# Scan stage: the three taps of each projection's shift placed apart, two R pieces behind a correction

## The chip, the cores and the metric

The kernel runs on one core of one Trainium2 chip. The metric is the device time of one execution in microseconds (us), and the median of the runs is compared. An execution of the kernel before takes about 3002 us; the profile is that of one further execution.

## What is computed

The kernel computes two transformer blocks on 512 tokens of 1024 channels. The change touches one stage of the first block only, the token mixer's recurrent scan. Cut to what matters:

```python
def centred_shift(z, w):                      # three taps along the tokens
    zp = jnp.pad(z, ((0, 0), (1, 1), (0, 0)))
    return zp[:, :-2] * w[0] + zp[:, 1:-1] * w[1] + zp[:, 2:] * w[2]

z = h @ p["w_in"]                             # r, k, v of every head, of 512 tokens and 256 context tokens
r, k, v, ... = split(centred_shift(z_rwkv, shift_conv))
def step(S, inp):                             # generalised delta rule, forward and reverse, per head
    s_kk = einsum('bhvk,bhk->bhv', S, kk_t)
    S_new = S * d_t - s_kk * (kk_t * a_t) + v_t * k_t
    y = einsum('bhvk,bhk->bhv', S if reverse else S_new, r_t)
```

After the scan come its readout, a gated merge, a mixture of experts, and the second block (two attention mixers). They are the same in both kernels.

## The kernel before

`stage_scan` treats the 1024 channels as 8 blocks of 128 (two heads each). The tokens are cut in 12 steps of 64 (4 of context, 8 of the sequence), in both directions. Inside a step the recurrence is turned into a triangular system; its inverse is built for groups of 4 steps by 5 levels of correction. Between steps a 64x64 state is carried.

**Turns and slots.** The loop runs over turns j = 0 to 8. A turn has three groups s of five levels l, so 15 corrections, each with two half slots; the text writes a half slot as (s, l, 0) or (s, l, 1), and a correction as (s, l). A turn takes about 100 us. In it three channel blocks are in work: j gets its inverses, the state steps go through the end of block j-1 (s = 0) and the beginning of j, and block b = j+1 is prepared: its projections, shifts, decays, rates and scores. For b to exist j is 0 to 6.

**One correction, on four engines.** All instruction streams are written out by hand and run in their written order; they meet at semaphores. PE: `product` (it waits for the inverse of the level before), the right side of a state step with the scores beside it, then what `beside(j, (s, l, 0))` gives, `solve` (waits for the negated right side), `correct` (waits for the mask), `read_out` (waits for the copied solution), then `beside(j, (s, l, 1))`. DVE: `mask` (L1548), `beside` 0, `update` (L1559 of X, L1561 of XT), `state` (L1574, and L1578 for the scaled ZG), `beside` 1. ACT: `negate` (L1218), `beside` 0, `solved` (L1223), `beside` 1. In a group's last level PE runs `correct_last` (L825, and L828, which turns the next group's start matrix XT); L828 waits for POOL's `xt0`, two instructions (L1476, L1478), and these wait for ACT's `part_moved` (L1276, two instructions), which waits until DVE's `parts` has masked all scores of that group's steps.

**Projections and shifts.** PE projects block b in pieces (L684; the context's K and V at L680) into one PSUM bank, in the order K_X, K_V, R_X, V_X; the next projection waits until the shift of the one before has read the bank. DVE's `shift(b, which)` reads the bank with three taps: a product (L400, for K_V L1604), and two multiply-adds (L403, L406; for K_V L1607, L1610). Each counts a semaphore, `shift`. K_V is two parts of 256 tokens, so its taps are six instructions; the others have three on 512 tokens. Behind the last tap of K_V wait ACT's `square(b)` (L1287, 128x768, in half slot (1, 2, 1)), POOL's reversal of v and PE's R_X projection.

**Where things stand before.** On DVE: `parts(j, 4..11)` one each in (s, 0..3, 0) for s = 0, 1; `shift(b, K_X)` in (0, 3, 0); `shift(b, K_V)` in (1, 2, 1); `gated(a)` (L1725) in (1, 3, 0); `parts(b, 0)`, `parts(b, 2)` (L1638) and `shift(b, R_X)` in (2, 2, 1); `scaled_r(b)` in (2, 3, 1). On PE: pieces 0 and 1 of R_X in (1, 3, 0), `squares(b)` (L695) in (1, 3, 1), piece 2 in (1, 4, 0). On ACT: `square(b)` in (1, 2, 1), `part_moved(j, 2)` in (1, 3, 1), `part_moved(b, 0)` in (2, 3, 0), ahead of `solved` of that slot, `part_moved(j, 1)` in (0, 3, 1).

Of the kernel before, what the change touches and what calls it, by code (L numbers as in the profile page):

```python
# [7 lines left out]
ALU = mybir.AluOpType  # L8
# [4 lines left out]
T, TC, D = 512, 256, 1024  # L13
# [383 lines left out]
def shifted(own, dve, parts, w):  # L397

    for dst, z, n in parts:
        own.then(dve.tensor_scalar(dst, z, w[1], None, ALU.mult))  # L400
    own.settle()
    for dst, z, n in parts:
        own.then(dve.scalar_tensor_tensor(dst[:, 1:n], z[:, 0:n - 1], w[0], dst[:, 1:n], ALU.mult, ALU.add))  # L403
    own.settle()
    for dst, z, n in parts:
        own.then(dve.scalar_tensor_tensor(dst[:, 0:n - 1], z[:, 1:n], w[2], dst[:, 0:n - 1], ALU.mult, ALU.add))  # L406
    own.settle()
# [106 lines left out]
def stage_scan(k, hT, w_low, low_loaded, th, da, sg, ya, spare, m, first_chunk, first_loaded, loose):  # L514
# [20 lines left out]
    with ExitStack() as s:  # L535
# [70 lines left out]
        SHIFTED = 15  # L606
# [20 lines left out]
        def _(pe):  # L627
# [363 lines left out]
            def beside(j, at):  # L991

                a, b = j - 1, j + 1
                if at == (0, 0, 0):
                    turn_params(b)
                if at == (0, 0, 1):
                    project(b, K_X, 0)
                if at == (0, 1, 0):
                    project(b, K_X, 1)
                    bonus(j)  # L1000
                if at == (0, 1, 1):
                    project(b, K_X, 2)
                if at == (0, 2, 1):
                    project(b, K_X, 3)
                if at == (0, 2, 0):
                    both_directions(b, "rate")
                if at == (0, 3, 0):
                    both_directions(b, "decay")
                if at == (0, 3, 1):
                    to_tokens(j, "B", 0)  # L1010
                if at == (0, 4, 0):
                    context_of(b, 0)
                    to_tokens(j, "K", 0)
                if at == (0, 4, 1):
                    context_of(b, 1)
                    center(a)
                    project(b, K_V, 0)
                if at == (1, 0, 0):
                    variance(a)
                if at == (1, 0, 1):  # L1020
                    project(b, K_V, 1)
                if at == (1, 1, 0):
                    project(b, K_V, 2)
                    spread_rstd(a)
                if at == (1, 1, 1):
                    project(b, K_V, 3)
                if at == (1, 2, 1):
                    gate(a)
                if at == (1, 3, 0):
                    project(b, R_X, 0, KT)  # L1030
                    project(b, R_X, 1, KT)
                if at == (1, 3, 1):
                    squares(b)
                if at == (1, 4, 0):
                    project(b, R_X, 2, KT)
                if at == (1, 4, 1):
                    project(b, R_X, 3, KT)
                if at == (2, 0, 0):
                    spread_inverse(b)
                if at == (2, 0, 1):  # L1040
                    project(b, R_X, 4, KT)
                if at == (2, 1, 0):
                    project(b, R_X, 5, KT)
                if at == (2, 1, 1):
                    project(b, R_X, 6, KT)
                if at == (2, 2, 0):
                    project(b, R_X, 7, KT)
                if at == (2, 2, 1):
                    scores(b, 0)
                    scores(b, 2)  # L1050
                if at == (2, 3, 1):
                    for i in range(3):
                        project(b, V_X, i, KT)
                if at == (2, 4, 0):
                    for i in range(3, 5):
                        project(b, V_X, i, KT)
                if at == (2, 4, 1):
                    for i in range(5, KT):
                        project(b, V_X, i, KT)
# [480 lines left out]
        def _(dve):  # L1540
# [43 lines left out]
                    sc.settled(dve, "par", j)  # L1584
                    ts(col(j, 18), col(j, 10), -1.0, 1.0, ALU.mult, ALU.add).then_inc(S["par_done"], 1)

            def shift(j, which):

                if not live(j):
                    return  # L1590
                dve.wait_ge(S["proj"], proj_no(j, which))
                mine = Steps(dve, S["shift"], shift_no(j, which - 1) if which else SHIFTED * j)
                taps_of = lambda i: [col(j, 3 * t + i) for t in range(3)]
                z_of = proj_bank(j, which)
                if which == K_X:
                    if j:
                        dve.wait_ge(S["ke_done"], 2 * j)
                    shifted(mine, dve, [(kj[:, XS], z_of[:], T)], taps_of(1))
                elif which == K_V:
                    if j:  # L1600
                        sc.settled(dve, "tokV", j - 1, 0)
                    parts_ = ((kj[:, CS], z_of[:, 0:TC], taps_of(1)), (vj[:, CS], z_of[:, TC:2 * TC], taps_of(2)))
                    for dst, z, w in parts_:
                        mine.then(ts(dst, z, w[1], None, ALU.mult))  # L1604
                    mine.settle()
                    for dst, z, w in parts_:
                        mine.then(stt(dst[:, 1:TC], z[:, 0:TC - 1], w[0], dst[:, 1:TC], ALU.mult, ALU.add))  # L1607
                    mine.settle()
                    for dst, z, w in parts_:
                        mine.then(stt(dst[:, 0:TC - 1], z[:, 1:TC], w[2], dst[:, 0:TC - 1], ALU.mult, ALU.add))  # L1610
                    mine.settle()
                elif which == R_X:
                    shifted(mine, dve, [(rj[:], z_of[:], T)], taps_of(0))
                else:
                    if j:
                        sc.settled(dve, "tokV", j - 1, 1)
                        sc.settled(dve, "tokV", j - 1, 2)
                    shifted(mine, dve, [(vj[:, XS], z_of[:], T)], taps_of(2))

            def bonus(j):  # L1620
                if live(j):
# [104 lines left out]

            def beside(j, at):
                a, b = j - 1, j + 1
                if at[0] < 2 and at[1] < 4 and at[2] == 0:
                    parts(j, 4 + 4 * at[0] + at[1])  # L1730
                if at == (0, 0, 0):
                    params(b)
                if at == (0, 1, 1):
                    bonus(j)
                if at == (0, 3, 0):
                    shift(b, K_X)
                if at == (1, 0, 0):
                    inverse_deviation(a)
                if at == (1, 0, 1):
                    running_sums(b, 0)  # L1740
                if at == (1, 1, 1):
                    normed(a)
                if at == (1, 2, 1):
                    shift(b, K_V)
                if at == (1, 3, 0):
                    gated(a)
                if at == (1, 3, 1):
                    clamp(b)
# [10 lines left out]
                    scaled_q(b, 0)  # L1759
                if at == (2, 2, 1):  # L1760
                    parts(b, 0)
                    parts(b, 2)
                    shift(b, R_X)
                if at == (2, 3, 1):
                    scaled_r(b)
                if at == (2, 4, 0):
# [1919 lines left out]
```

## Time and profile before

| | us |
|---|---|
| median of 3 runs | 3002.47 (3000.74 to 3004.83) |
| the profiled execution's own time | 3004.26 |
| its span, first to last instruction | 3002.5 |
| scan, turns 0 to 7 | about 125 to 908 on the span's clock |

The page of the profile gives busy shares over the span: PE 91%, DVE 39%, ACT 20%, POOL 8%. In the timeline a row has the start, the duration, the engine (PE matmul, PEld weight load, DVE, ACT, POOL), the line and operation, how many instructions are merged in the row, and in brackets the idle time ahead of it with what ended it ("<-DVE vj L1610": an instruction of DVE at line 1610 that wrote vj). "issue" is idle time for which the profile shows no wait. [...]

### The profile page before, as it was taken

What the parts mean: (1) busy time and instruction counts of PE and PEld (TensorE: products, weight loads), DVE (VectorE), ACT (ScalarE), POOL (GpSimd) and SP (SyncE); (2) the same over time, 40 slices, a digit from 0 to 9 for tenths busy, and PEclk for the clock granted to TensorE, in tenths of its full rate; (3) what the DMA queues carried; (4) which work ended last, traced back from release to release, by engine and by line L of the source; (5) the groups of instructions that cost most, each with busy time, mean ns of one, the idle gap of its engine ahead of it and who ended that gap; (6) DMA issues with size and microseconds to landing.
All of it is one profiled execution on the core that took longest, in us unless ns stands there. A gap on an engine that the chain in (4) does not pass through costs nothing. (4 is left out here: it accounts for less than half of the span.)

```text
span 3002.5 us, 69531 instructions
## 1 busy us (share of the span) xinstructions
PE 2732.5 (91%) x31106; PEld 1482.5 (49%) x31106; DVE 1182.1 (39%) x2613; ACT 608.2 (20%) x1255; POOL 250.1 (8%) x282
## 2 busy tenths in 40 slices
PE   6899999999999899988998989989887999899998
PEld 3566666776664445444433433433333455455553
DVE  3565566566643673163221211212013245423333
ACT  3233233333321100010000000000002344322222
POOL 1121122112200000001000000000000021110000
PEclk9999999999999999998999999999997999999999
DMA  5000000000005773167999999999995421042210
GB/s 204 24 26 14 19 26 20 21 19 26 12 26 196 279 282 113 56 273 297 430 431 431 430 431 430 431 431 430 431 431 196 134 71 37 0 123 63 63 42 29
DMA packets 191501, 557.42 MB, mean 186 GB/s; under 512 B 32140, under 2 KB 119714, under 8 KB 166646
## 3 DMA queue, kind: packets, MB, share of 16 engines
q1 hardware_dynamic: 191222, 553.19, 47.0%
q8 instruction: 237, 3.88, 0.5%
q14 instruction: 42, 0.34, 0.0%
HBM read 550.65 MB, written 2.24 MB: 184 GB/s over the span
## 5 line engine op out<-in xcount | busy, mean ns | idle before, releaser
L2327 PE MATMUL bank<-arena,xe 128*64 128x512 f32 x1024 | 345.2, 601 | 35.0 <-DMA gates<-in_exp_w_dram 24.0
L684 PE MATMUL bank<-arena 128*128 128x512 f32 x384 | 201.5, 647 | 6.7 <-DVE vj L1610 5.3
L2327 PEld LDWEIGHTS bank<-arena,xe 128*64 128x64 f32 x1024 | 107.9, 138 | 183.1 <-issue 170.4
L3354 PE MATMUL bank<-arena 128*128 128x512 f32 x384 | 176.2, 607 | 3.4 <-PEq L3232 3.4
L2327 PE MATMUL bank<-arena,hidT 128*64 128x512 f32 x512 | 171.7, 599 | 2.4 <-DMA gates<-in_exp_w_dram 1.9
L2780 PE MATMUL bank<-arena 128*128 128x512 f32 x320 | 143.3, 596 | 0.0
L2327 PE MATMUL bank<-mg_ring,xe 128*64 128x512 f32 x256 | 117.9, 615 | 20.9 <-DMA u<-in_exp_w_dram 20.9
L2552 DVE TENSOR_TENSOR x<-x,bank 128x512 f32<-128x512 f32 x64 | 43.7, 686 | 227.6 <-PE bank L2365 227.6
L2545 DVE TENSOR_TENSOR hid<-hid,bank 128x512 f32<-128x512 f32 x32 | 19.8, 682 | 285.4 <-PE bank L2327 285.4
L2327 PE MATMUL bank<-ys,xe 128*64 128x512 f32 x256 | 114.5, 600 | 19.1 <-DMA arena<-in_exp_w_dram 18.5
L1548 DVE TENSOR_TENSOR pm<-bank,m_level 128x512 f32<-128x512 f32 x120 | 82.7, 689 | 118.1 <-PE bank L763 117.1
L843 PE MATMUL bank<-pm,XT 64*64 64x32 f32 x3072 | 107.0, 219 | 12.6 <-DVE pm L1548 10.7
L2327 PE MATMUL bank<-u,xe 128*64 128x512 f32 x256 | 118.2, 616 | 0.0
L2327 PE MATMUL bank<-gates,xe 128*64 128x512 f32 x256 | 117.9, 615 | 0.0
L845 PE MATMUL bank<-XT,pm 64*64 64x32 f32 x3072 | 110.8, 221 | 1.7 <-issue 1.7
L3354 PEld LDWEIGHTS bank<-arena 128*128 128x128 f32 x384 | 70.9, 192 | 84.0 <-issue 84.0
L763 PEld LDWEIGHTS bank<-X,px 64*64 64x64 f32 x2560 | 84.9, 134 | 49.5 <-issue 22.5
L843 PEld LDWEIGHTS bank<-pm,XT 64*64 64x64 f32 x3072 | 99.7, 136 | 17.1 <-DVE pm L1548 12.9
L763 PE MATMUL bank<-X,px 64*64 64x64 f32 x2560 | 97.1, 223 | 7.5 <-issue 4.8
L845 PEld LDWEIGHTS bank<-XT,pm 64*64 64x64 f32 x3072 | 99.5, 135 | 0.6 <-issue 0.5
L684 PEld LDWEIGHTS bank<-arena 128*128 128x128 f32 x384 | 67.8, 197 | 63.7 <-issue 57.9
L183 DVE SCALAR_TENSOR_TENSOR arena<-ws_w,silu_c,arena 128x512 f32<-128x512 f32 x120 | 90.2, 752 | 12.5 <-DMA ws_w<-in_ada_w_dram 7.5
(530 smaller groups left out, 5471.7 us busy)
## 6 DMA issues: line engine op xcount, KB each, us to landing
arena<-in_exp_w_dram SPq DMA_DIRECT2D x96, 2048.0 KB, 26.8
gates<-in_exp_w_dram SPq DMA_DIRECT2D x24, 2048.0 KB, 29.6
ys<-in_exp_w_dram SPq DMA_DIRECT2D x24, 2048.0 KB, 26.7
mg_ring<-in_exp_w_dram SPq DMA_DIRECT2D x24, 2048.0 KB, 25.7
u<-in_exp_w_dram SPq DMA_DIRECT2D x24, 2048.0 KB, 30.2
ws_w<-in_ada_w_dram SPq DMA_DIRECT2D x40, 1024.0 KB, 5.2
arena<-in_odd_w_in_dram SPq DMA_DIRECT2D x32, 512.0 KB, 3.9
arena<-in_w_in_dram SPq DMA_DIRECT2D x24, 512.0 KB, 4.2
```

Of the source, the lines that this page charges most:

```text
L183: own.last(dve.scalar_tensor_tensor(acc, w, factor, acc, ALU.mult, ALU.add))
L684: last = mm(to[:], wj[:, c, i, :], hT[:, c, 0:T], start=(c == 0), stop=(c == KT - 1))
L763: last = mm(INV[c, cs(q)], part(4 * g + q // 2, q % 2, 0, 0)[h], X[h, (j * GROUPS + g) % 2, q, :], start=True, stop=True)
L843: mm(into(INV, h, q), XT[c, g, q, :], blocks(pm[c, q, :], b, 0), start=True, stop=True)
L845: last = mm(into(INVT, c, q), pm[c, q, :], blocks(XT[c, g, q, :], b, 1), start=True, stop=True)
L1548: tt(pm[:], INV[:].rearrange("p (q t) -> p q t", q=8), m["level"][:, l, :].unsqueeze(1).to_broadcast([P, 8, HEAD]), ALU.mult).then_inc(S[" ...
L2327: r[e] = mm(out[a, :], lhs[j][:, a], w[:, j, 512 * c:512 * c + 512], start=(first and j == 0), stop=(last and j == len(lhs) - 1), skip_gro ...
L2545: dve.tensor_tensor(hid[:, f, :], hid[:, f, :], bank[4 + f][:], ALU.mult).then_inc(S["hid_made"], 1)
L2552: dve.tensor_tensor(x1[:, n, c], x1[:, n, c], bank[scatter_bank(q, o)][:], ALU.add).then_inc(S["added"], 1)
L2780: last = mm(o[:], w[:, c, i, :], hT[:, i, :], start=(i == 0), stop=(i == KT - 1))
L3354: last = mm(o[:], w[:, i, t, :], hT[:, t, :], start=(t == 0), stop=(t == KT - 1))
```

## The change

Nothing is computed otherwise; instructions of DVE and PE stand in other places.

- DVE's `shift` takes the taps to be done. K_X: tap 0 in (0, 2, 1), tap 1 in (0, 3, 0), tap 2 in (0, 3, 1). K_V: tap 0 in (1, 2, 0), tap 1 in (1, 2, 1), tap 2 in (1, 3, 0), ahead of `gated(a)`. R_X: taps 0 and 1 in (2, 2, 1), tap 2 in (2, 3, 0). V_X and the prologue keep all three together.
- DVE's `parts(j, 11)` goes from (1, 3, 0) to (1, 3, 1), `parts(b, 2)` from (2, 2, 1) to (2, 3, 0), behind tap 2 of R_X.
- PE's pieces 0 and 1 of R_X go from (1, 3, 0), ahead of `solve` and `correct`, to (1, 3, 1), behind them and ahead of `squares(b)`.

```diff
@@ PE, beside
-                if at == (1, 3, 0):
+                if at == (1, 3, 1):
                     project(b, R_X, 0, KT)
                     project(b, R_X, 1, KT)
-                if at == (1, 3, 1):
                     squares(b)
@@ DVE, shift
-            def shift(j, which):
+            def shift(j, which, taps=range(3)):
...
+                mine = Steps(dve, S["shift"], (shift_no(j, which - 1) if which else SHIFTED * j) + taps[0] * len(parts_))
+                if taps[0] == 0:
+                    dve.wait_ge(S["proj"], proj_no(j, which))
...
+                for tap in taps:
+                    if tap:
+                        mine.settle()
+                    for dst, z, w, n in parts_:
+                        if tap == 0:
+                            mine.then(ts(dst, z, w[1], None, ALU.mult))
+                        elif tap == 1:
+                            mine.then(stt(dst[:, 1:n], z[:, 0:n - 1], w[0], dst[:, 1:n], ALU.mult, ALU.add))
+                        else:
+                            mine.then(stt(dst[:, 0:n - 1], z[:, 1:n], w[2], dst[:, 0:n - 1], ALU.mult, ALU.add))
+                mine.settle()
@@ DVE, beside
-                if at[0] < 2 and at[1] < 4 and at[2] == 0:
+                if at[0] < 2 and at[1] < 4 and at[2] == (1 if at[0:2] == (1, 3) else 0):
                     parts(j, 4 + 4 * at[0] + at[1])
...
+                if at == (0, 2, 1):
+                    shift(b, K_X, (0,))
                 if at == (0, 3, 0):
-                    shift(b, K_X)
+                    shift(b, K_X, (1,))
+                if at == (0, 3, 1):
+                    shift(b, K_X, (2,))
...
+                if at == (1, 2, 0):
+                    shift(b, K_V, (0,))
                 if at == (1, 2, 1):
-                    shift(b, K_V)
+                    shift(b, K_V, (1,))
                 if at == (1, 3, 0):
+                    shift(b, K_V, (2,))
                     gated(a)
...
                 if at == (2, 2, 1):
                     parts(b, 0)
+                    shift(b, R_X, (0, 1))
+                if at == (2, 3, 0):
+                    shift(b, R_X, (2,))
                     parts(b, 2)
-                    shift(b, R_X)
```

## Rows read from the trace of the kernel before

**Rows 1.** The page, part 1: engine, busy us (share), instructions.
```profile
PE 2732.5 (91%) x31106; PEld 1482.5 (49%) x31106; DVE 1182.1 (39%) x2613; ACT 608.2 (20%) x1255; POOL 250.1 (8%) x282
```

**Rows 2.** Busy time by stretch, turn 6: us, engines in order, granted clock.
```profile
727.00:825.00 98.00, 91.84 (x2781) 67.32 (x2777) 61.63 (x126) 34.01 (x70) 18.77 (x15) 1.00 0.04 11
```

**Rows 3.** What PE's matmuls waited for, 125 to 908 us: total us, times, longest.
```profile
PE bank L843 <- DVE pm L1548: 10.7, 12, 1.7
PE bank L763 <- DVE XT L1561: 8.1, 16, 1.1
PE bank L684 <- DVE vj L1610: 5.3, 7, 0.8
PE bank L763 <- issue: 5.1, 5, 2.2
```

**Rows 4.** Timeline, turn 6, corrections (1, 3) and (1, 4), picked rows.
```profile
780.72 0.47 DVE L1610 SCALAR_TENSOR_TENSOR vj<-bank,pcol,vj 128x255 f32<-128x255 f32 x1
781.23 0.94 ACT L1287 ACTIVATE x<-kj,pcol 128x768 f32<-128x768 f32 x1 [4.77 <-DVE vj L1610]
781.34 1.96 PE L684 MATMUL bank<-arena 128*128 128x512 f32 x4 [0.83 <-DVE vj L1610]
781.84 0.68 DVE L1632 TENSOR_TENSOR px<-bank,m_part 128x512 f32<-128x512 f32 x1
782.07 0.26 ACT L1218 ACTIVATE x<-bank 128x128 f32<-128x128 f32 x1
...
784.02 1.27 ACT L1276 ACTIVATE XT<-px 64x512 f32<-64x512 f32 x2
...
785.84 0.95 DVE L1578 TENSOR_TENSOR ZG<-Z,g 128x128 f32<-128x128 f32 x1
786.72 1.27 POOL L1478 TENSOR_TENSOR XT<-XT,m_id 128x512 f32<-128x512 f32 x1
...
788.09 0.25 PE L825 MATMUL bank<-XT,pm 64*64 64x32 f32 x2 [0.41 <-issue]
```

**Rows 5.** Timeline, turn 7, correction (1, 4).
```profile
875.12 1.27 POOL L1478 TENSOR_TENSOR XT<-XT,m_id 128x512 f32<-128x512 f32 x1
...
876.49 0.25 PE L825 MATMUL bank<-XT,pm 64*64 64x32 f32 x2
```

**Rows 6.** Timeline, turn 2, corrections (2, 2) and (2, 3), picked rows.
```profile
409.34 0.75 DVE L1638 TENSOR_TENSOR pc<-bank,m_part 128x256 f32<-128x256 f32 x2 [0.18 <-PE bank L725]
...
410.88 1.27 ACT L1276 ACTIVATE XT<-pc 64x512 f32<-64x512 f32 x2
...
412.06 0.25 ACT L1223 ACTIVATE x<-bank 128x128 f32<-128x128 f32 x1
...
412.36 0.69 DVE L1548 TENSOR_TENSOR pm<-bank,m_level 128x512 f32<-128x512 f32 x1
...
413.10 0.25 PE L843 MATMUL bank<-pm,XT 64*64 64x32 f32 x2 [1.74 <-DVE pm L1548]
...
414.07 0.61 PE L932 MATMUL bank<-x 64*64 64x64 f32 x8
```

**Rows 7.** Timeline, turn 5, corrections (0, 3) and (0, 4), picked rows.
```profile
650.47 0.75 DVE L406 SCALAR_TENSOR_TENSOR kj<-bank,pcol,kj 128x511 f32<-128x511 f32 x1
...
652.06 0.27 PE L763 MATMUL bank<-X,pc 64*64 64x64 f32 x2 [0.83 <-DVE XT L1561]
...
652.75 1.27 POOL L1478 TENSOR_TENSOR XT<-XT,m_id 128x512 f32<-128x512 f32 x1
...
654.31 0.27 PE L828 MATMUL bank<-m_id,XT 64*64 64x64 f32 x2
```

**Rows 8.** Busy time by stretch, turn 2, columns as in rows 2.
```profile
412.00:414.00 2.00, 0.90 (x61) 0.90 (x64) 1.01 (x2) 0.31 (x2) 1.70 (x2) 1.00 0.00 0
414.00:416.00 2.00, 2.00 (x27) 1.33 (x21) 1.66 (x5) 0.00 (x0) 2.00 (x2) 0.54 0.04 8
```

**Rows 9.** PE timeline, the same V_X pieces at (2, 3, 1), turn 2 and turn 6.
```profile
414.62 4.29 PE L684 MATMUL bank<-arena 128*128 128x512 f32 x6
...
812.90 2.84 PE L684 MATMUL bank<-arena 128*128 128x512 f32 x6
```

More of the change, by code:

```diff
@@ L1585, in params @@
                     ts(col(j, 18), col(j, 10), -1.0, 1.0, ALU.mult, ALU.add).then_inc(S["par_done"], 1)
-            def shift(j, which):
+            def shift(j, which, taps=range(3)):
                 if not live(j):
                     return
-                dve.wait_ge(S["proj"], proj_no(j, which))
-                mine = Steps(dve, S["shift"], shift_no(j, which - 1) if which else SHIFTED * j)
-                taps_of = lambda i: [col(j, 3 * t + i) for t in range(3)]
+                w_of = lambda i: [col(j, 3 * t + i) for t in range(3)]
@@ L1594, in shift @@
                 z_of = proj_bank(j, which)
                 if which == K_X:
-                    if j:
+                    parts_ = ((kj[:, XS], z_of[:], w_of(1), T),)
+                elif which == K_V:
+                    parts_ = ((kj[:, CS], z_of[:, 0:TC], w_of(1), TC), (vj[:, CS], z_of[:, TC:2 * TC], w_of(2), TC))
+                elif which == R_X:
+                    parts_ = ((rj[:], z_of[:], w_of(0), T),)
+                else:
+                    parts_ = ((vj[:, XS], z_of[:], w_of(2), T),)
@@ L1597, in shift @@
+                mine = Steps(dve, S["shift"], (shift_no(j, which - 1) if which else SHIFTED * j) + taps[0] * len(parts_))
+                if taps[0] == 0:
+                    dve.wait_ge(S["proj"], proj_no(j, which))
+                    if which == K_X and j:
                         dve.wait_ge(S["ke_done"], 2 * j)
-                    shifted(mine, dve, [(kj[:, XS], z_of[:], T)], taps_of(1))
-                elif which == K_V:
-                    if j:
+                    if which == K_V and j:
@@ L1601, in shift @@
                         sc.settled(dve, "tokV", j - 1, 0)
[L1602 to L1615, printed above, removed]
+                    if which == V_X and j:
                         sc.settled(dve, "tokV", j - 1, 1)
                         sc.settled(dve, "tokV", j - 1, 2)
-                    shifted(mine, dve, [(vj[:, XS], z_of[:], T)], taps_of(2))
+                for tap in taps:
[6 more added lines that the diff above has]
+                            mine.then(stt(dst[:, 1:n], z[:, 0:n - 1], w[0], dst[:, 1:n], ALU.mult, ALU.add))
+                        else:
+                            mine.then(stt(dst[:, 0:n - 1], z[:, 1:n], w[2], dst[:, 0:n - 1], ALU.mult, ALU.add))
```

## The prediction

> **What bounds the kernel now.** I read the page's busy shares first: PE is busy 91% of the span, all others under 40% [rows 1]. Next came the stretches of the scan, one by one turn: turn 6 has 92 of 98 us of PE work at the full clock, DVE 62, ACT 34, POOL 19 [rows 2]. So PE sets the pace, and only what makes PE stand still, or work at the lower clock, can move the time. The third view is the list of what PE's matmuls waited for in the scan [rows 3]. Three of its lines are the ones the change aims at: 10.7 us for a mask (`correct` waits for L1548), 8.1 us for an update (`product` waits for L1561), 5.3 us for the end of K_V's shift (R_X's first piece waits for L1610). In the timeline they lie at fixed places: the mask in (2, 3), 1.74 us in turns 0, 1, 2, 3 and 6 and 0.6 and 0.4 us in 4 and 5 (turn 2 is shown) [rows 6]; the update in (0, 4), 0.83 us in most turns [rows 7]; K_V's shift in (1, 3), 0.83 us in six turns and 0.4 us in turn 0 [rows 4]. That is about 20 us. The question at each place is what is late next, since in each slot ACT and POOL have chains that end within tenths of a microsecond of PE's arrival.
>
> **(1, 3): R's pieces go behind the correction.** Turn 6 as the pattern [rows 4]. PE ends the right side at 781.34 - 0.83 = 780.51. Then it waits for the shift, does pieces 0 and 1 (1.96 us), and starts `solve` at about 783.3, when the negated right side has long been there: ACT negates at 782.07 to 782.33, and it does so behind `square(b)` (781.23 for 0.94 us), which waited for K_V's last tap, as its idle time says. After the change that last tap ends no earlier. Two tap instructions of 0.47 us leave the row ahead of it (0.9 us), but one mask (0.61 us from its start to the next, plus an estimated 0.1 us of waiting for the product) comes in: 781.19 - 0.9 + 0.7 = about 781.0, against 781.19. ACT's order isn't touched: square to 782.0, negate to 782.2. So PE has nothing to do from 780.5 until about 782.25, because the pieces that covered this now stand behind it. It idles 1.74 us, where it idled 0.83 here and 0.17 behind `squares`. The pieces cost the same 1.96 us behind the correction. Loss: 1.74 - 1.00 = **0.75 us** a turn, some 5 us in 7 turns. With the pieces' cover gone, the wait that the change was to remove is replaced by one on ACT's `square`.
>
> **(1, 4): the moved `parts(j, 11)`.** Before, it runs at 781.84, ahead of the update. ACT's `part_moved(j, 2)` then starts at 784.02, right behind `solved`, takes 1.27 us, POOL's two instructions take 1.27 us each and end at 787.99, and PE starts `correct_last` at 788.09, 0.1 us later, after a gap of 0.41 us. The profile calls the gap "issue", but POOL's end explains it, as it does in turns 4 and 5 at the same 0.1 us. So this chain already ends last here. After the change `solve` starts at 782.25 and not 783.3, correction and `read_out` end at 783.85, and DVE does X, XT (0.35 us each to the next start), Z (0.5) and ZG (0.2, no longer beside POOL) and then `parts` (0.68): done at 785.8 or so. ACT 785.8 to 787.1, POOL 787.15 to 789.75, `correct_last` at 789.85 in place of 788.09. That is **1.8 us** a turn for both places together. Before I take it for every turn: in turns 1 to 3 the product of (1, 4) is cut by an "issue" pause of 1.3 to 2.2 us (2.2 is the longest) [rows 3], so `correct_last` comes late anyway and POOL's chain is hidden; there only the 0.75 us of (1, 3) count. Turn 0 lacks most of the 0.83 us wait and loses 2.1. Turn 7 has no R pieces; `parts(7, 11)` moves all the same, POOL's chain ends last there too (876.39 against 876.49 [rows 5]), and it loses the way from the old start of `part_moved` to the new one, 2.7 us. Sum: 2.1 + 3 x 0.75 + 3 x 1.8 + 2.7 = **+12.5 us**.
>
> **(2, 3): R_X's shift apart.** Before, DVE does two `parts` and three taps, so the mask comes at 412.36 and `correct` at 413.10 after 1.74 us [rows 6]. After, `parts(b, 2)` (0.75) and a tap (0.75) are gone from in front of it: mask at 410.7, ready at 411.35, `correct` at 411.4, ready at 412.5. The wait is gone. What is late next: `part_moved(b, 0)` waits for `parts(b, 2)` and stands on ACT ahead of `solved`. Before, it ran at 410.88 to 412.15, with `solved` right behind it at 412.06, all hidden under the mask's wait. After, `parts(b, 2)` comes behind mask and tap 2: 410.7 + 0.61 + 0.79 + 0.75 = 412.8. Then 1.27 us of `part_moved` and 0.25 us of `solved` end at 414.3, and `read_out` starts there, where it started at 414.07. So 1.7 us are won and 1.95 lost: **+0.25 us**. In turns 4 and 5 the product of (2, 3) is itself late by a pause; there the mask had cost 0.6 and 0.4 us only, while the new chain (mask, tap, parts, two ACT instructions and one more, 3.7 us) starts at the product's end: +1.1 and +0.9. Sum 5 x 0.25 + 2.0 = **+3.2 us**.
>
> POOL's `xt0(b, 0)` and the longer product behind it move back by 2 us, beside `scaled_r`. ZG (128x128) takes 0.95 us beside L1476 in turn 6, more than the mask's 0.68 us over four times as many elements, and ends as POOL goes over to L1478 at 786.72 [rows 4]. If both products of `scaled_r` are held like that, the mask of (2, 4) comes up to 0.5 us late, ahead of a `correct_last` that two V_X pieces precede (two pieces are 1.96 us in rows 4, the mask 0.7): nothing. [...]
>
> **(0, 4): K_X's shift apart.** Tap 0 goes ahead of the mask of (0, 3), tap 2 ahead of that of (0, 4); there DVE waits for a product for longer than a tap's 0.75 us, so both cost nothing. The update starts 1.2 us sooner (0.75 for tap 0 and the rest of the row up to PE's end), so the product's wait of 0.83 us goes [rows 7]. But `correct_last` needs POOL's L1478, which ends at 654.02 and doesn't move; PE now starts at 654.31 and can't before 654.1. Gain **0.2 us** a turn, 0.4 in turn 0: **-1.6 us**. Its bounds are 0 and the whole 0.83 x 7 = 5.8 us.
>
> **The clock.** [...] Bounds: 0, and one fall in each of 8 turns, 11.6 us. I take one fall's price, **+1.5 us**, nearer to the low end for that hiding.
>
> **Sum.** 12.5 + 3.2 - 1.6 + 1.5 = +15.6 us. On the profiled execution that is 3004.3 + 15.6 = 3019.9; it stood 1.8 us above the median, so against the median of 3002.5: **3018 us**.
>
> **The rivals.**
> 1. *The chain of ACT in (1, 3), (1, 4) is as I say, but pauses take part of it (chance 0.12, about 3006).* The "issue" pauses are 5.1 us at L763 alone and some 20 us in the list as a whole. If PE's instructions keep arriving while it waits, the new waits swallow pauses that stood elsewhere; with half of the 20 us and no fall of the clock, 3002.5 + 14 - 10 = 3006.5, within 0.2%. For it: the pauses sit at changing places from turn to turn. Against: turns 4 to 6 have few of them near the two places.
> 2. *Nothing is late next (0.06, 2982).* ACT and POOL have more slack than the rows let me see, and the three waits just go: 3002.5 minus about 20. It decides at (1, 3): `negate` would have to be ready within 0.1 us of the right side's end, though `square` can't start before K_V's last tap. The rows speak against it in all seven turns.
> 3. *Each new wait pulls the clock down (0.12, 3028).* Eight falls at 1.45 us, unhidden, in place of one: 3018 + 10. For it: the clock fell after four of five waits of 1.74 us.
> 4. *My own case (0.70, 3009 to 3024).*
>
> **How the numbers follow.** A difference of 0.2%, 6 us, is about what a measurement tells from none. Slower by more: my case and the third rival, 0.82; within: the first, 0.12; faster: 0.06. The range takes in my case, most of the third and a part of the first: 3006 to 3028.
>
> **What would show it.** In the profile after: K_V's last tap ends just as late behind the right side, L905 of (1, 3) idles about 1.7 us for L1218; L1276 of group 2 starts behind `parts` and L1478 ends 0.1 us before L825 in turns 0, 4 to 7, with 1 us and more of idle PE; L843 of (2, 3) no longer waits, L932 does, for L1223, 1.7 us; L763 of (0, 4) doesn't wait and L828 does. Wrong I am if L905 in (1, 3) doesn't wait, or if the mask's line in the list of waits shrinks with no new line for L932 and L905.

## The result and the profile after

The kernel after takes 3020.9 us (median, 3018.89 to 3023.45), the kernel before 3003.65 beside it (3000.74 to 3006.75): a ratio of 1.006, 95% interval 1.0044 to 1.0076. It is slower by 17 us, 15.6 were forecast. The profiled execution took 3020.28 us, its span is 3018.5, 16.0 longer than before.

Page, part 1, of the kernel after:

```profile
PE 2746.4 (91%) x31106; PEld 1487.5 (49%) x31106; DVE 1176.8 (39%) x2613; ACT 608.9 (20%) x1255; POOL 255.2 (8%) x282
```

Against [rows 1] no engine got or lost an instruction. PE is busy 13.9 us longer although it does the same matmuls: 2.1 us of it ahead of the first mask, 9.3 in the scan and 2.5 behind. In the scan PE stands idle only 5.6 us more than before, so a good part of the loss is matmuls that took longer, among them those at the lower clock. In the list of what PE's matmuls waited for, 125 to 925 us (total us, times, longest), the first three lines of [rows 3] are small or gone and three others have grown. PE's line numbers are those of before; the others differ by one to some tens (L1217 is `negate`, L1222 `solved`, L1547 the mask, L1560 the update, L1634 and L1640 `parts`, L1275 `part_moved`, L1475 and L1477 POOL's `xt0`, L1286 the square).

```profile
PE bank L905 <- ACT x L1217: 18.3, 27, 1.8
PE bank L932 <- ACT x L1222: 14.4, 16, 1.8
PE bank L825 <- issue: 10.7, 12, 3.0
...
PE bank L763 <- DVE XT L1560: 1.4, 2, 0.8
```

The same three in the kernel before, 125 to 908 us:

```profile
PE bank L905 <- ACT x L1218: 5.6, 20, 0.4
PE bank L932 <- ACT x L1223: 3.8, 9, 0.5
...
PE bank L825 <- issue: 2.1, 4, 0.9
```

The wait for the mask is down from 10.7 us to 0.9, that for the update from 8.1 to 1.4, that for K_V's shift is gone: the change does what it says. In their place PE waits 18.3 us for the negated right side (`solve`, L905), 14.4 for the copied solution (`read_out`, L932) and 10.7 ahead of `correct_last` (L825). Timeline of turn 6, corrections (1, 3) and (1, 4), to be held against [rows 4]:

```profile
793.33 0.47 DVE L1619 SCALAR_TENSOR_TENSOR vj<-bank,pcol,vj 128x255 f32<-128x255 f32 x1
793.84 0.93 ACT L1286 ACTIVATE x<-kj,pcol 128x768 f32<-128x768 f32 x1 [4.71 <-DVE vj L1619]
794.68 0.26 ACT L1217 ACTIVATE x<-bank 128x128 f32<-128x128 f32 x1
794.99 0.39 PE L905 MATMUL bank<-x,XT 64*64 64x64 f32 x6 [1.82 <-ACT x L1217]
797.81 0.68 DVE L1634 TENSOR_TENSOR px<-bank,m_part 128x512 f32<-128x512 f32 x1
798.68 1.27 ACT L1275 ACTIVATE XT<-px 64x512 f32<-64x512 f32 x2 [2.92 <-DVE px L1634]
800.03 1.27 POOL L1475 TENSOR_TENSOR XT<-XT,m_pair 128x512 f32<-128x512 f32 x1 [5.77 <-ACT XT L1275]
801.38 1.26 POOL L1477 TENSOR_TENSOR XT<-XT,m_id 128x512 f32<-128x512 f32 x1
802.74 0.25 PE L825 MATMUL bank<-XT,pm 64*64 64x32 f32 x2 [1.62 <-issue]
```

ACT has been idle for 4.71 us when K_V's last tap ends; then it does the square first, because it is written first, and only then the 0.26 us of `negate` that PE stands waiting for. Below that the second chain: `parts` at 797.81, ACT at 798.68, POOL from 800.03 to 802.64, `correct_last` at 802.74, after 1.62 us of idle PE. `correct_last` starts 0.10 us behind POOL's end in all eight turns of the kernel after. In the kernel before it does so in turns 4 to 7 only; in turns 0 to 3 POOL was done 0.43, 1.15, 2.14 and 2.52 us earlier.

Turn 7 of the same chain, against [rows 5], and (2, 3) of turn 2, against [rows 6]:

```profile
891.49 1.26 POOL L1477 TENSOR_TENSOR XT<-XT,m_id 128x512 f32<-128x512 f32 x1
892.85 0.25 PE L825 MATMUL bank<-XT,pm 64*64 64x32 f32 x2 [2.98 <-issue]
```

```profile
415.94 0.25 PE L843 MATMUL bank<-pm,XT 64*64 64x32 f32 x2
416.58 0.76 DVE L1640 TENSOR_TENSOR pc<-bank,m_part 128x256 f32<-128x256 f32 x2
417.42 1.27 ACT L1275 ACTIVATE XT<-pc 64x512 f32<-64x512 f32 x2 [2.00 <-DVE pc L1640]
418.59 0.25 ACT L1222 ACTIVATE x<-bank 128x128 f32<-128x128 f32 x1
418.90 0.45 PE L932 MATMUL bank<-x 64*64 64x64 f32 x8 [1.56 <-ACT x L1222]
```

`correct` (L843) no longer waits for its mask, but ACT starts `part_moved` only behind `parts(b, 2)`, and the copy of the solution stands behind it.

**Where the 16 us are.** There are 15 masks in a turn, at the same places in both kernels. The differences of the times from one mask to the next, in us, after minus before, summed over the turns (a row takes in the stretches that start at the masks of the corrections it names):

| place | forecast | measured |
|---|---|---|
| up to the first mask (prologue) | 0 | +2.7 |
| (0, 0) to (0, 2) | 0 | -2.0 |
| (0, 3), (0, 4) | -1.6 | -2.7 |
| (1, 0), (1, 1) | 0 | +0.2 |
| (1, 2) to (1, 4) | +12.5 | +12.3 |
| (2, 0), (2, 1) | 0 | +0.3 |
| (2, 2) to (2, 4) | +3.2 | +6.8 |
| clock | +1.5 | (inside the rows above) |

Behind the last mask -1.6 us, so 16.0. By turns (1, 2) to (1, 4) is +1.63, 1.45, 1.05, -0.22, 2.08, 0.78, 1.99, 3.52. The clock is inside (2, 2) to (2, 4): turns 4 and 5 lose 2.95 and 2.35 us there, turns 0 to 3 and 6 0.27 to 0.38, turn 7 nothing. A stretch of two us in turn 4 (busy time of PE, PEld, DVE, ACT, POOL; granted clock; DMA):

```profile
626.00:628.00 2.00, 2.00 (x4) 0.90 (x3) 1.51 (x1) 0.00 (x0) 2.00 (x2) 0.53 0.00 0
```

The granted clock is a share of PE's full clock: 0.53 over these two us, 0.50 in the one from 625 to 626 us. So PE is at half its clock under the V_X pieces, as in [rows 8], in a turn where it had not happened before. Read from 100 us to the end of the scan in stretches of one us, the time at half the clock is 30.7 us before (10.2 around the end of the prologue, six falls of 3.4) and 47.8 after (10.2 and eleven falls of 3.4).

### The profile page after: what moved, and what is told of

Read it like the earlier page. It is cut to its first block and busy times, and to the rows that moved or that the text cites. A ratio compares the mean times of both kernels' runs of the same rounds, so it can differ in the third digit from the quotient of the medians.

```text
span 3018.5 us, 69553 instructions
## 1 busy us (share of the span) xinstructions
PE 2746.4 (91%) x31106; PEld 1487.5 (49%) x31106; DVE 1176.8 (39%) x2613; ACT 608.9 (20%) x1255; POOL 255.2 (8%) x282
## 5 line engine op out<-in xcount | busy, mean ns | idle before, releaser
L1547 DVE TENSOR_TENSOR pm<-bank,m_level 128x512 f32<-128x512 f32 x120 | 82.9, 691 | 116.0 <-PE bank L763 115.3
L843 PE MATMUL bank<-pm,XT 64*64 64x32 f32 x3072 | 107.7, 219 | 2.7 <-issue 1.3
L763 PEld LDWEIGHTS bank<-X,px 64*64 64x64 f32 x2560 | 85.6, 135 | 47.2 <-issue 21.8
L843 PEld LDWEIGHTS bank<-pm,XT 64*64 64x64 f32 x3072 | 100.2, 136 | 7.4 <-issue 3.5
L763 PE MATMUL bank<-X,px 64*64 64x64 f32 x2560 | 97.9, 224 | 4.3 <-issue 2.8
```

The lines of the kernel that those rows point to most:

```text
L763: last = mm(INV[c, cs(q)], part(4 * g + q // 2, q % 2, 0, 0)[h], X[h, (j * GROUPS + g) % 2, q, :], start=True, stop=True)
L843: mm(into(INV, h, q), XT[c, g, q, :], blocks(pm[c, q, :], b, 0), start=True, stop=True)
L1547: tt(pm[:], INV[:].rearrange("p (q t) -> p q t", q=8), m["level"][:, l, :].unsqueeze(1).to_broadcast([P, 8, HEAD]), ALU.mult).then_inc(S[" ...
```

## The experiments

My theory: the change takes away three waits, and in (1, 3), (1, 4) and (2, 3) the next thing late is a copy on ACT that stands behind a long ACT instruction, and the chain `parts`, `part_moved`, POOL. The rivals: PE's pauses swallow most of it; or the lower clock is most of it. Ratios are against the kernel before, measured again beside each group of runs (medians 3005.7, 3003.4 and 3002.9 us), with their 95% intervals; between two groups they say more than the times. Each trace is of one execution. "Mask to mask" is the difference by place as in the table above.

**One part undone: `parts(j, 11)` back.** The kernel after with `parts(j, 11)` in (1, 3, 0) again, behind tap 2.

```diff
-                if at[0] < 2 and at[1] < 4 and at[2] == (1 if at[0:2] == (1, 3) else 0):
+                if at[0] < 2 and at[1] < 4 and at[2] == 0 and at[0:2] != (1, 3):
...
                     shift(b, K_V, (2,))
+                    parts(j, 11)
                     gated(a)
```

> The changed kernel with parts(j, 11) alone put back into half slot (1, 3, 0), behind tap 2 of K_V and ahead of gated(a). My theory: the chain parts, part_moved, POOL's two products, correct_last sets the time of (1, 4), and moving parts behind the state made it 1 us longer in turns 0, 4, 5, 6 and 2.7 us in turn 7. So the gaps at L825 (1.63 us in turns 5 and 6, 2.97 us in turn 7 of the changed kernel) go to under 0.6 us, the wait of L905 for ACT at (1, 3) stays at 1.8 us, and the time falls by about 7 us against the changed kernel, to 3014. Rival: the gaps at L825, which the profile puts down to issue, are instructions that arrive late; then they stay, and the time stays at 3021.

Measured 0.9994 (0.9985 to 1.0003), 3004.3 us: the whole loss is gone, where I had expected less than half. The waits, same stretch:

```profile
PE bank L905 <- ACT x L1217: 19.1, 29, 1.8
PE bank L932 <- ACT x L1222: 13.6, 18, 1.8
...
PE bank L825 <- issue: 1.8, 6, 0.6
```

L825 falls from 10.7 us to 1.8, the other two stay. Mask to mask (1, 2) to (1, 4) gains 13.6 us on the kernel after: 0.09, 2.34, 1.19, 1.08, 2.47, 1.49, 1.70, 3.26 by turns. My error was in turns 1 to 3: I had left POOL's chain out there because a pause of 1.3 to 2.2 us cut the product before it. In the kernel after those pauses are 0.75, 0.2 and 0 us, so POOL's chain ends last in these turns too. With the rest of the change in place, moving one DVE instruction of 0.68 us a turn makes the whole difference.

**One part undone: the R pieces back.** The kernel after with pieces 0 and 1 in (1, 3, 0).

```diff
-                if at == (1, 3, 1):
+                if at == (1, 3, 0):
                     project(b, R_X, 0, KT)
                     project(b, R_X, 1, KT)
+                if at == (1, 3, 1):
                     squares(b)
```

> The changed kernel with PE's pieces 0 and 1 of R_X alone put back ahead of solve and correct in (1, 3, 0). My theory: the wait of L905 for ACT at (1, 3) (1.8 us a turn) goes, L684 waits about 0.7 us for K_V's last tap, but all of correct, read_out, state and the parts behind it come 0.9 us later, so POOL's chain ends later and the gap at L825 grows from 1.63 to about 3.1 us in turns 5 and 6. Net +0.85 us in four turns, -0.75 us in three: about 3022, the same as the changed kernel. Rival: the two pieces are the whole loss of (1, 3); then 7 turns x 0.75 us come back, and the time is 3015 or 3016 with L825 as in the changed kernel.

Measured 1.0093 (1.0078 to 1.0109), 3036.0 us: 15 us above the kernel after by the medians, 10 by the ratios, where I had expected one. Waits, and POOL's chain in turn 6:

```profile
PE bank L825 <- issue: 20.0, 14, 3.3
...
PE bank L684 <- DVE vj L1620: 5.5, 7, 0.8
PE bank L905 <- ACT x L1218: 4.5, 17, 0.4
```

```profile
814.30 1.26 POOL L1478 TENSOR_TENSOR XT<-XT,m_id 128x512 f32<-128x512 f32 x1
815.66 0.25 PE L825 MATMUL bank<-XT,pm 64*64 64x32 f32 x2 [3.28 <-issue]
```

The sizes of the waits are as expected (0.8 us for the shift again, 3.3 us at L825 in turns 4 to 6). Two things came on top. The pauses in turns 1 to 3 returned (1.9, 1.6, 1.2 us). And each gap of 3.3 us is followed by a fall of the clock: 71.6 us at half the clock from 100 us to the end of the scan. So the pieces' move, which I had costed as a loss of 0.75 us a turn by itself, is a gain once `parts(j, 11)` stands where the change puts it: with the pieces ahead of `solve` PE has their 1.96 us [rows 4] less to do between `solve` and `correct_last`, and stands there for POOL instead (3.28 us against 1.62 in turn 6).

**The pieces' move alone.** The kernel before with that one edit.

```diff
-                if at == (1, 3, 0):
+                if at == (1, 3, 1):
                     project(b, R_X, 0, KT)
                     project(b, R_X, 1, KT)
-                if at == (1, 3, 1):
                     squares(b)
```

> The kernel before with PE's pieces 0 and 1 of R_X alone moved behind the correction of (1, 3). My theory: L905 waits 1.87 us for ACT's L1218 behind square, where 0.83 and 0.17 us were lost before, so +0.87 us a turn, 6 us in all; correct_last of (1, 4) comes 0.7 us later, PE-bound and not POOL-bound. The pauses in turns 1 to 3 (5.3 us) may be swallowed by the new wait, and falls of the clock may be added: ratio 1.002, at most 1.004. Rival: the pieces' move wins the 0.83 us wait for K_V's shift, ratio 0.998.

Measured 0.9994 (0.9982 to 1.0005), 3001.7 us: no change, where I had expected 1.002. Waits, and `solve` in turn 3:

```profile
PE bank L905 <- ACT x L1217: 18.5, 29, 1.9
...
PE bank L763 <- issue: 1.2, 1, 1.2
```

```profile
481.68 0.39 PE L905 MATMUL bank<-x,XT 64*64 64x64 f32 x6 [1.88 <-ACT x L1217]
```

The new wait is there at its full size, 1.88 us. But L763's "issue" line falls from 5.1 us [rows 3] to 1.2: the pauses of 1.3 to 2.2 us ahead of (1, 4) are gone, and turns 2 and 3 gain 1.68 and 2.88 us mask to mask where they should have lost 0.75. (Turns 1 and 6, where a fall of the clock is new, lose 0.77 and 3.42.) Here the first rival's sum is right: the pauses that went pay for the new wait. Its reason, that PE waits earlier, is not shown, for the pauses go with the place of the pieces. In turns 1 to 3 they are 0.7 to 2.4 us in each of the six kernels here that have the pieces ahead of `solve`, and 0 to 0.9 us in each of the eight that have them behind the correction, also where `solve` waits for 0.4 us at most (with the square moved 0 in all three turns, in the mended kernel 0.54, 0.88 and 0.35).

**K_X apart alone.** The kernel before, with `shift`'s argument and the taps of K_X where the change puts them.

```diff
+                if at == (0, 2, 1):
+                    shift(b, K_X, (0,))
                 if at == (0, 3, 0):
-                    shift(b, K_X)
+                    shift(b, K_X, (1,))
+                if at == (0, 3, 1):
+                    shift(b, K_X, (2,))
```

> The kernel before with only K_X's taps apart (tap 0 in (0, 2, 1), tap 1 in (0, 3, 0), tap 2 in (0, 3, 1)). My theory: the wait of L763 for DVE's update in (0, 4) (0.83 us a turn) goes, and correct_last of (0, 4) waits for POOL's L1478 in its place for about 0.6 us, so only 0.2 us a turn are won: 3002, no difference from the kernel before. Rival: POOL isn't in the way and the whole 0.83 us x 6 are won, 2998.

Measured 0.9988 (0.9978 to 0.9997), 3003.7 us. (0, 3) and (0, 4) gain 0.27 us a turn, 0.2 were forecast; the update's wait goes from 8.1 us to this:

```profile
PE bank L763 <- DVE XT L1561: 2.3, 8, 0.7
```

A wait of 0.83 us taken away gives 0.27, because POOL's `xt0` ends when it did: L828 starts 0.1 us behind it in six of the eight turns, where it was mostly 0.3 us before.

**R_X apart alone.** The kernel before, with taps 0 and 1 of R_X in (2, 2, 1), tap 2 and `parts(b, 2)` in (2, 3, 0).

```diff
                 if at == (2, 2, 1):
                     parts(b, 0)
-                    parts(b, 2)
-                    shift(b, R_X)
+                    shift(b, R_X, (0, 1))
+                if at == (2, 3, 0):
+                    shift(b, R_X, (2,))
+                    parts(b, 2)
```

> The kernel before with only R_X's shift and parts(b, 2) apart (taps 0 and 1 in (2, 2, 1), tap 2 and parts(b, 2) in (2, 3, 0)). My theory: correct no longer waits for the mask in (2, 3) (1.74 us), read_out waits as long for ACT's L1223, which stands behind part_moved; 0.25 us more in five turns and 1 us in turns 4 and 5, about +3 us, and up to +6 us where the clock falls in more turns than before: 3006 to 3010. Rival: ACT has slack there and the mask's wait of 10.7 us in all goes: 2993.

Measured 1.0025 (1.0016 to 1.0034), 3012.1 us. The wait and its place in turn 2:

```profile
PE bank L932 <- ACT x L1223: 13.9, 19, 1.8
```

```profile
410.07 1.27 ACT L1276 ACTIVATE XT<-pc 64x512 f32<-64x512 f32 x2 [2.00 <-DVE pc L1641]
411.25 0.25 ACT L1223 ACTIVATE x<-bank 128x128 f32<-128x128 f32 x1
```

The profiled execution has the same 30.7 us at half the clock as the kernel before, so it shows the mechanism without the clock: (2, 2) to (2, 4) loses 0.24, 0.16, 0.29, 0.30, 1.24, 0.64 and 0.29 us, 3.2 in all, the forecast's sum, with the two larger values in turns 4 and 5 as forecast. That execution took 3005.9 us, though, the lowest of its kernel; the others took 3010 to 3014. What the rest cost in those, no trace shows.

**ACT mended at (2, 3).** The kernel after with `part_moved(b, 0)` behind `solved`.

```diff
@@ ACT, beside
-                if at == (2, 3, 0):
+                if at == (2, 3, 1):
                     part_moved(b, 0)
```

> The changed kernel with one ACT step moved: part_moved(b, 0) from half slot (2, 3, 0), where it stands ahead of solved, to (2, 3, 1), behind it. My theory: the wait of L932 for L1222 in (2, 3) (1.8 us in five turns, 0.9 us in two) is only this order, so it goes; POOL's products for XT start 1.3 us later than in the kernel before and end long before correct_last of (2, 4). That gives -10.8 us, and the six falls of the clock behind that wait (1.45 us each) go too: about -19 us against the changed kernel, ratio to the kernel before about 0.9995. Without an effect on the clock it would be -11 us, ratio 1.002. Rival: U is late because solve is late, then nothing changes, ratio 1.006.

Measured 0.9987 (0.9977 to 0.9996), 3001.5 us.

```profile
PE bank L932 <- ACT x L1222: 4.6, 11, 0.5
```

The wait of 14.4 us is 4.6, and (2, 2) to (2, 4) gains 20.5 us on the kernel after: 3.2 to 3.5 in turns 0 to 3, which is the wait of 1.6 to 1.8 us and a fall of the clock with its 1.45 us [rows 9] behind it. In turns 4 and 5 it is 3.1 and 3.0, of which the waits are only 0.96 and 0.77: that leaves some 2.2 us each for the fall. 47.8 us at half the clock become 34.2.

**ACT mended at (1, 3).** The kernel after with `square(b)` behind `solved`.

```diff
@@ ACT, beside
-                if at == (1, 2, 1):
+                if at == (1, 3, 1):
                     square(b)
```

> The changed kernel with one ACT step moved: square(b) from (1, 2, 1), ahead of negate of (1, 3), to (1, 3, 1), ahead of part_moved(j, 2). My theory: L905's wait of 1.8 us in (1, 3) is negate standing behind square, which waits for K_V's last tap; it falls to 0.4 us. The chain over parts(j, 11) starts 1.35 us sooner, so correct_last of (1, 4) comes 1.35 us sooner in turns 0 to 6, and turn 7 doesn't change: -9.5 us against the changed kernel, ratio about 1.003. In turns 1 to 3 pauses of late instructions may come back ahead of (1, 4) (1 to 2 us each), since PE no longer stands still before them. Rival: the wait is for the right side itself, ratio 1.006.

Measured 1.0013 (1.0003 to 1.0023), 3008.0 us.

```profile
PE bank L825 <- issue: 15.1, 14, 2.9
...
PE bank L905 <- ACT x L1217: 7.7, 29, 0.4
```

`solve` waits 0.4 us at most: it was the square. But L825 rises from 10.7 to 15.1, with 1.3 to 1.6 us in turns 0 to 6: of the 18.3 - 7.7 = 10.6 us won at L905, 4.4 are passed on to the next wait. Mask to mask (1, 2) to (1, 4) gains 11.1 us on the kernel after; what lies above 10.6 - 4.4 = 6.2 is pauses and clock, which I can't split.

**All three.** The kernel after with both ACT moves and `parts(j, 11)` back in (1, 3, 0); the three diffs stand above.

> The changed kernel with all three found steps mended: part_moved(b, 0) to (2, 3, 1), square(b) to (1, 3, 1), parts(j, 11) back in (1, 3, 0) behind tap 2 of K_V. My theory: against the kernel before each turn wins about 1.0 us at (1, 3), 0.4 us at (1, 4) in the clean turns, 1.7 us at (2, 3) in five turns and 0.5 us in two, 0.2 us at (0, 4), 20 us in all, and the falls of the clock behind (2, 3) are gone, 4 x 1.45 us: ratio 0.992, about 2981 us. Rival: what is won at these places is given back by late instructions and by POOL's chain; then ratio 0.997 or more.

Measured 0.9898 (0.988 to 0.9916), 2974.0 us: 30 us faster than the kernel before, 47 than the kernel after, and better than the 0.992 that I had expected. Waits, and `solve` in turn 6:

```profile
PE bank L905 <- ACT x L1217: 7.7, 29, 0.4
PE bank L932 <- ACT x L1222: 5.4, 14, 0.5
...
PE bank L825 <- issue: 2.1, 5, 0.9
```

```profile
752.01 0.28 ACT L1217 ACTIVATE x<-bank 128x128 f32<-128x128 f32 x1 [4.00 <-PE bank L865]
752.34 0.39 PE L905 MATMUL bank<-x,XT 64*64 64x64 f32 x6 [0.19 <-ACT x L1217]
...
753.01 0.93 ACT L1286 ACTIVATE x<-kj,pcol 128x768 f32<-128x768 f32 x1
```

All three new waits are small, and the time at half the clock is 10.3 us (6.8 around the end of the prologue and one fall). Against the kernel before (1, 2) to (1, 4) gains 12.8 us, (2, 2) to (2, 4) 12.4, (0, 0) to (0, 2) 2.0, (0, 3) and (0, 4) 1.4.

**The two ACT moves without the change.** The kernel before with the two ACT diffs only.

> The kernel before with the two ACT steps moved as in the mended kernel (square(b) to (1, 3, 1), part_moved(b, 0) to (2, 3, 1)), and nothing of the change. My theory: in the kernel before ACT has slack at both places, because PE waits for DVE there (K_V's last tap, the mask of (2, 3)), so these two steps alone win nothing: ratio 0.999 to 1.001. The 1% of the mended kernel would then come only from both together. Rival: ACT's order was the loss all along, ratio 0.995 or less.

Measured 1.0009 (0.9998 to 1.002), 3007.2 us.

```profile
PE bank L843 <- DVE pm L1548: 10.2, 12, 1.7
```

The mask's wait of [rows 3] stands as it was, and so does that for the shift (5.3 us), and there is no gain. The move of the square also has a price here: it now stands ahead of `part_moved(j, 2)`, and L825 waits 1.22, 1.13 and 1.22 us in turns 4 to 6 in place of 0.41. So the 1% belongs to neither half. With `parts(j, 11)` left where it was, the change without the ACT moves gives 0.9994, the ACT moves without the change 1.0009, and both together 0.9898.

**The pieces' move with ACT mended.** The mended kernel with the two R pieces back in (1, 3, 0).

> The mended kernel with PE's pieces 0 and 1 of R_X back in (1, 3, 0). My theory: with square out of the way negate is ready 0.35 us behind the right side, so the pieces cover nothing any more; in (1, 3, 0) they wait 0.75 us for K_V's last tap, in (1, 3, 1) they wait for nothing. So 0.4 us a turn are lost at (1, 3), and as correct comes later POOL's chain may show at (1, 4) again by some tenths: ratio 0.991 to 0.9935, against 0.9898 of the mended kernel. Rival: the pieces' place makes no difference, 0.990.

Measured 0.9964 (0.9951 to 0.9978), 2992.8 us; I had expected 0.991 to 0.9935.

```profile
PE bank L763 <- issue: 7.5, 9, 2.2
...
PE bank L825 <- issue: 6.0, 10, 1.2
PE bank L684 <- DVE vj L1620: 5.3, 7, 0.8
```

Without the move the shift's wait is back (5.3 us), L825 waits 1.22 us in turns 4 to 6, and pauses of 1.9 to 2.35 us in turns 1 to 3. Putting the pieces behind the correction is thus worth about 19 us here, against nothing in the kernel before. And since `solve` waits 0.4 us at most in both kernels, the pauses came back with the pieces' place alone. Five more falls of the clock in the scan came with them, in the one execution that was traced.

**Filling the two waits.** To see whether the clock stays up when PE works in the two waits, without a change of order, I put matmuls of zeros with weights of zeros (128x128, into a bank that they leave as it is) ahead of `solve` in (1, 3) and of `read_out` in (2, 3), ten in each place, in turns 0 to 6. They add work to PE and nothing to the result.

```diff
+            def fill():
+                for _ in range(FILLERS):
+                    mm(Y[:, 0:P], nought[:], hT[:, 0, 0:P], start=False, stop=True, skip_group_check=True)
...
+                            if (s, l) == (1, 3) and live(j + 1):
+                                fill()
                             solve(sj, n + l)
                             correct(j, s, l)
+                            if (s, l) == (2, 3) and live(j + 1):
+                                fill()
                             read_out(sj, n + l)
```

> The changed kernel with ten added matmuls of 128x128 (stationary operand zero, so they add nothing; 1.3 us in all) in the two new waits of PE: ahead of solve in (1, 3) and ahead of read_out in (2, 3), turns 0 to 6. They change no order and no wait. If the falls of the clock follow from these waits, and cost 1.5 us each in the median run as well, then the falls in (1, 4) and (2, 3) go (nine of 3.4 us in the changed kernel's profile), and the time falls by 8 to 13 us, ratio 1.002 to 1.0035, though turns 4 and 5 lose 0.4 us each in (2, 3). If the clock has no part in the loss, the ratio stays at 1.006 or rises to 1.0065.

Measured 1.0066 (1.0047 to 1.0085), 3023.8 us. The ten fillers ahead of `read_out` in (2, 3) of turn 6; each matmul stands in the trace as two records:

```profile
825.30 2.50 PE L901 MATMUL bank<-arena,nought 128*128 128x128 f32 x20
```

`read_out` starts 2.43 us behind the first of them, so ten took longer than the wait of 1.8 us that they were to fill: one costs 0.24 us and I had reckoned with 0.13. The time at half the clock fell from 47.8 us to 17.1, but 0.6 us and more of delay at each of the 14 places stands against it, so this run can't tell what the clock costs. With seven in each place, again in turns 0 to 6:

> The kernel of run filled with seven added matmuls in each place instead of ten: ten took 2.4 us, longer than the waits of 1.8 us, and lost 0.5 to 0.6 us at most of 14 places; seven should take 1.7 us and fit, but for (2, 3) in turns 4 and 5, where the wait is 0.9 us (1.5 us lost in all). If the falls of the clock cost time, the ratio to the kernel before falls from the changed kernel's 1.006 to 1.003 or 1.004. If they cost nothing in sum, it stays at 1.006.

Measured 1.005 (1.0036 to 1.0064), 3015.6 us, and 30.7 us at half the clock, of which 10.2 around the end of the prologue. The interval overlaps that of the kernel after: it points the way of the clock's price, and no more. One thing the trace does show (L827 is `correct_last` here):

```profile
PE bank L827 <- issue: 14.9, 13, 3.0
```

It waits 14.9 us, against 10.7 in the kernel after, and in (1, 4) 1.6 us in six of the seven turns with fillers. The falls of the clock in (1, 3) are gone, and PE only comes to wait longer for POOL's chain.

## Why the prediction was right

**(1, 3), +0.75 us a turn: right.** L905 waits 1.81 to 1.83 us in all seven turns, 1.74 forecast, for the reason forecast: moving the square away took it to 0.4.

**(1, 4), POOL's chain: the chain right, one reason for leaving it out wrong.** +12.3 us for both places against 12.5. Turn 6 lost 1.99 us (1.8 forecast) and turn 7 3.52 (2.7 forecast; a fall of the clock follows at 894 us). The step that failed is that a pause in turns 1 to 3 hides the chain. The pauses shrank once the pieces stood behind the correction, the chain showed, and the two nearly cancelled: 1.45, 1.05 and -0.22 against 0.75 each. Putting `parts(j, 11)` back brought out what had cancelled. Turn 0 lost 1.63 against 2.1 (POOL had 0.43 us in hand there before, which the forecast left out), and turn 5 only 0.78 against 1.8, because a pause of 0.93 us ahead of L828 went too. That the sum agrees to 0.2 us is luck: turns miss by up to 1 us either way, and the 12.3 us also hold what the falls of the clock in turns 0, 4 and 7 cost there.

**(2, 3), +3.2 us: the mechanism right to the tenth** in the kernel with R_X alone. In the kernel after it is +6.8. The difference is in turns 4 and 5, 1.7 us more in each, where the clock falls and didn't in the kernel with R_X alone.

**(0, 4), -1.6 us: 2.7 gained,** inside its bounds. 1.8 of it lie in turns 0 to 6; the rest is in turn 7, where nothing was moved in (0, 4).

**The clock, +1.5 us: mis-sized.** The term is one fall's price: in the kernel before the same V_X pieces took 4.29 us in turn 2, with the granted clock at 0.54 over two us of them, and 2.84 in turn 6, at 1.00 [rows 8, 9], 1.45 us apart. The fall followed the mask's wait of 1.74 us in (2, 3) in turns 0 to 3 and not in turn 6. No run shows that the change costs one fall: in the trace of the kernel after there are five falls more in the scan. Two of them cost their whole price (turns 4 and 5 of (2, 3)); two, in (1, 3) of turns 0 and 4, lie ahead of `correct_last`'s wait for POOL, which hides part of it, the hiding that the term was kept low for (in turn 4 L825 then waits 0.39 us in place of 1.63); the fifth comes in turn 7, behind L825. A second reading doesn't need the places in the trace: over all executions of all kernels here, taken within each kernel, 0.001 less of the mean granted clock goes with 1.6 us more time (correlation 0.7). The kernel after stands at 0.9708 on average, the kernel before at 0.9733 to 0.9737: (0.9735 - 0.9708) x 1600 = an estimate of +4.3 us. A third is PE's busy time: it grows by 6.3 us in turns 4, 5 and 7, which have four of the five new falls; but it also grows by 2.9 in turns 0 to 3, with no more time at half the clock than before, so 6.3 is too much for the clock alone. An estimate for the term is thus 4 to 6 us in place of 1.5.

**Terms that no step of mine had.** (0, 0) to (0, 2) gains 2.0 us, 1.58 of it in turn 0. No pause does that: in the kernel before, the stretch at half the clock that starts in the prologue reaches 5.9 us into turn 0, in the kernel after 1.9 us, and every trace in which it reaches in for about 2 us has the same 1.6 us less there. The prologue's +2.7 lies ahead of anything that was moved; in the fourteen traces the first mask comes between 123.0 and 128.1 us. Behind the last mask 1.6 us are gained. Together they make -0.9 us. So 15.6 against 17 is in part luck: a clock term too small by some 3 us or more, against gains in the prologue's slow stretch, in turn 7 and behind the scan that no step forecast.

**The rivals.** The first (pauses take part of it) holds in its sum for the pieces' move alone, where they take everything, and in turns 1 to 3 of the kernel after, but not for the reason it gave: the pauses go with the pieces' place, whether PE waits earlier or not. It didn't decide because POOL's chain took up what it gave. The second (nothing is late next) falls for the kernel as it is, and its 2982 us are what the mended kernel reaches, and passes (2974), once ACT's order is right. The third (each new wait pulls the clock down) holds for (2, 3) in six of seven turns and for (1, 3) in three of seven.

**What stays open.** Why the pauses ahead of the (1, 4) product shrink or vanish when the two pieces stand behind the correction. Instructions that arrive late would be one reason for a pause, but nothing in the trace shows their arrival. And the clock's exact share of the 17 us, since the filled kernels couldn't separate it.

## What to carry to other kernels

A move that takes a wait away is worth what the next latest chain allows, so look, for each engine that PE meets just behind it, at what is written ahead of the small copy: here 0.93 us of square and 1.27 us of moved scores stood ahead of two copies of 0.25 us, harmless as long as PE was late itself. Splitting long work on one engine pays only if the engine that reads its pieces is put in order in the same step; here each half alone measured nothing, both together 1%. And keep the head of the longest chain (here one 0.68 us instruction, followed by 4 us on ACT and POOL) ahead of everything that can wait, and work without a deadline behind it.

## What the runs showed of the hardware

- In these runs the granted clock fell to 0.50 of the full one, for 3.4 us at a time, 6.8 in some places of the kernel with the R pieces back, behind many stops of PE of about 1.8 us and not behind others just as long: in the kernel after it followed the wait of 1.8 us in (2, 3) in turns 0, 1 and 3 and not in turn 6, and in (1, 3) in turns 0, 3 and 4 and not in 1, 2, 5 and 6. In (2, 3) of turns 4 and 5 it followed waits of only 0.96 and 0.77 us, with pauses of 0.4 to 1.05 us just ahead of them. After the 3.3 us gaps of the kernel with the R pieces back it came each time, and so it did after the gap of 2.9 to 3.0 us at L825 in turn 7 of every kernel that has one. Taking a wait of 1.6 to 1.8 us away gave 3.2 to 3.5 us where the fall went too.
- "issue" in the list of waits isn't always a pause of PE's own. At L825 it is the wait for POOL: in three places shown POOL's instruction ends at 802.64 and PE starts at 802.74, at 892.75 and 892.85, and 815.56 and 815.66.
- A 128x128 float32 matmul of zeros took 0.24 us at the full clock (granted 1.00 over the ten ahead of `read_out` in turn 6 of the first filled kernel), about twice what I had put down for it. It stands in the trace as two records 0.11 us apart, so a time for one record is half of the matmul's.
- ZG (L1578 before, 128x128) took 0.29 us by itself and up to 1.83 beside POOL; that it is stretched at all was in [rows 4], how far was not. The longest, in turn 6 of the kernel before:

```profile
813.28 2.35 POOL L1498 TENSOR_TENSOR kt<-kt,bt 128x1024 f32<-128x1024 f32 x1
813.95 1.83 DVE L1578 TENSOR_TENSOR ZG<-Z,g 128x128 f32<-128x128 f32 x1
```

POOL's product ends at 815.63, ZG at 815.78. In the same way each of the 22 ZG of the kernel before and the 7 of the kernel after that took over 0.35 us ends 0.15 us behind the end of a POOL instruction. In 125 to 925 us, count, then busy us and mean ns, before and after:

```profile
L1578 DVE TENSOR_TENSOR ZG<-Z,g 128x128 f32<-128x128 f32 x80 | 39.3, 492 | 2.8
```

```profile
L1577 DVE TENSOR_TENSOR ZG<-Z,g 128x128 f32<-128x128 f32 x79 | 26.7, 338 | 2.7
```

With the new order fewer of them lie beside a POOL instruction, and ZG takes 12.6 us less of DVE (all of DVE's work, by the page, 5.3 us less). No wait of PE in the lists is one for ZG.
